# A longer weight ring from the output projection on, and the last six feature blocks run token tile by token tile

## The chip, the cores and the metric

The kernel runs on all 8 cores of one Trainium2 chip, each core on its own share of the tokens, with no communication between cores. The metric is the device time in microseconds (us) of the slowest core.

The engines of a core have these short names: PE is TensorE (matmul), PEld its weight loads, DVE is VectorE, ACT is ScalarE, POOL is GpSimd and SP is SyncE. POOL and SP do no arithmetic here; they only issue DMAs.

## What is computed

One layer of a diffusion backbone on 16 context sequences of 256 tokens and 4 latent sequences of 2048 tokens, model width 2048. The part that the change touches is the end of the layer and the final norm. The reference, cut to it:

```python
def _rmsnorm(x, g):
    xf = x.astype(jnp.float32)
    y = xf * lax.rsqrt(jnp.mean(xf * xf, axis=-1, keepdims=True) + EPS)
    return (y * g.astype(jnp.float32)).astype(x.dtype)

def _layer(x, cond, h0, n_chunks, p):
    ...
    mix = jnp.concatenate([rg_out, ch_out], axis=-1) @ p['w_out']
    x = x + gate1 * mix
    h2 = _rmsnorm(x, p['norm2_g']) * (1.0 + scale2) + shift2
    ff = jnp.square(jax.nn.relu(h2 @ p['w_ff1'])) @ p['w_ff2']    # 2048 -> 8192 -> 2048
    x = x + gate2 * ff
    return x, ...

y_prompt = _rmsnorm(xp, final_g)
y_sample = _rmsnorm(xs, final_g)
```

The products run in bfloat16 with float32 sums; x, the norms and the outputs are float32.

## The kernel before

Each core owns 1536 tokens. Activations lie with features on the 128 partitions and tokens along the free dimension, so the model width of 2048 is 16 feature blocks `f` of 128. From the output projection on, the 1536 tokens are two groups `g` of 768 (`GRP`), and each group is two token tiles, `TILES = ((0, 512), (512, 256))`: first 512 tokens, then 256.

**Stages.** In order of the program: norm 1 and the first modulation blocks; the recurrent half (`oth_...`, `own_...`); the chunk-mixing half; `out_proj(0, ...)` and `out_proj(1, ...)`, which also sum up the squares for norm 2; then for each group `g` and each half `hf` of the 8192 hidden features, 16 blocks of the first feed-forward product (`ff1`, with weights of 16x256 columns) and 16 of the second (`ff2`, one feature block each, 32 accumulated products for each token tile). In the first `ff1` stage, after blocks 4 to 11, `mod_block(5, ...)` puts eight small products with a weight block of `w_ada` in between. After `ff2` with `hf == 1` the group is finished: final norm and store of 16 feature blocks.

**Weights.** All weight blocks come through one ring in SBUF, `RING`, of `NUNIT = 8` units of 4096 bytes a partition. A block of `w_out`, `w_ada`, `w_ff1` or `w_ff2` takes two units, so four blocks fit. A first pass over the program records the order of use. `acquire` hands the next block out, `release` frees it after its last product, and both call `ring_issue`, which issues the next load on POOL's queue as soon as `ring_free` finds room. A load's start therefore waits for the release of the block that it overwrites. The loads convert float32 in HBM to bfloat16 in SBUF.

**One `ff2` block before.** For each token tile: 32 products into one PSUM bank (`bank()` goes round over 8 banks), then on DVE `stt` adds the gated product to `xA` (the residual, float32), and with `hf == 1` `stat_add` squares it on ACT into `sq` and adds it on DVE to `ss`. Then the block is released.

**The end of a group before.** `stat_end` multiplies `ss` by a matrix of ones on PE for both tiles (a sum over partitions), takes the square root on ACT into `rs`, and one reciprocal on DVE over all 768 columns. Then DVE scales the 16 blocks of `xA` in place (768 columns each), and SP issues one store of 384 KB behind each. In group 0 this stands ahead of the evictions of group 1's first products on DVE; in group 1 nothing follows it.

**Order.** Every engine runs its instructions in the order in which this Python code calls them; the `Tracker` puts semaphore waits ahead of them from the byte ranges that they read and write. All matmuls are recorded at line 154, all DMAs at 173, activations at 309, `ts` at 314 and 316, `tt` at 319, `stt` at 323 and the reciprocal at 333.

**Memory around the change.** `X16` is a region of 16384 bytes a partition. It held x tiles, then parts of the recurrent buffers and the two buffers `gu[0]` and `gu[1]`, which the last chunk-mixing products read. From `out_proj` on nothing in the kernel before uses it.

Of the kernel before, what the change touches and what calls it, by code (L numbers as in the profile page):

```python
# [11 lines left out]
DM = 2048  # L12
# [193 lines left out]
def emit(nc, order):  # L206
# [145 lines left out]
    head = [0]  # L352
    live = []
    nxt = [0, 0]

    def ring_place(n):
        p = head[0]
        if p + n > NUNIT:
            p = 0
        return p  # L360

    def ring_free(p, n):
        used = sum(u for _, _, u in live)
        if not live:
            return True
        span = set()
        for _, q, u in live:
            span.update(range(q, q + u))
        return not any(k in span for k in range(p, p + n)) and used + n <= NUNIT

    def ring_issue():
        if order is None:
            return
        while nxt[0] < len(order):
# [3 lines left out]
            if not ring_free(p, n):  # L378
                free = [q for q in range(0, NUNIT - n + 1) if ring_free(q, n)]
# [3 lines left out]
            tile = at(RING + p * UNIT, [128, shp[0], shp[1]], BF16, "w_" + key[0])  # L383
# [6 lines left out]
    def acquire(kind, i):  # L390
        key = (kind, i)
        if order is None:
# [4 lines left out]
            return at(RING + p * UNIT, [128, shp[0], shp[1]], BF16, "w_" + kind), len(rec) - 1  # L397
# [446 lines left out]
    nbank[0] = 8  # L844

# [23 lines left out]

    def stat_end():  # L870
        for o_, n_ in TILES:
            p = bank()
            T.mm([(p[:, 0:n_], ones_f[:, :], ss[:, o_:o_ + n_], True, True)])
            act(rs[:, o_:o_ + n_], p[:, 0:n_], AF.Sqrt, bias=cst[:, 0:1], scale=1.0 / DM)
        recip(rs[:, :], rs[:, :])
# [40 lines left out]
    for g in range(2):  # L916
        for hf in range(2):
# [14 lines left out]
            if g == 1 and hf == 0:  # L932
                for f in range(16):
                    T.dma("sp", xA[:, f, :], x1s[f], f"xl{f}", ins=[f])
            for f in range(16):
                w, n = acquire("ff2", hf * 16 + f)
                for ti, (o_, n_) in enumerate(TILES):
                    p = bank()
                    T.mm([(p[:, 0:n_], w[:, k, :], aT[:, k, o_:o_ + n_], k == 0, k == 31) for k in range(32)])
                    x_ = xA[:, f, o_:o_ + n_]  # L940
                    stt(x_, p[:, 0:n_], ec(modT, 5, f, te(g, ti)), x_, ALU.mult, ALU.add)
                    if hf == 1:
                        stat_add(x_, f == 0, o_, n_)
                release(n)
        stat_end()
        for f in range(16):
            stt(xA[:, f, :], xA[:, f, :], pkc("FG", f), rs[:, :], ALU.mult, ALU.mult)
            T.dma("sp", y_own[f * 128:(f + 1) * 128, g * GRP:(g + 1) * GRP], xA[:, f, :], f"y{f}", final=True)
# [144 lines left out]
```

How the kernel before makes its waits and increments, by code:

```python
    def need(self, eng, tok):  # L72
        if tok is None:
            return
        sid, val, src = tok
        if eng == "pe" and src == "pe":
            return
        if self.waited[eng].get(sid, 0) >= val:
            return
        self.waited[eng][sid] = val
        h = self.sems[sid]
        self.q[eng].append(lambda E, h=h, v=val: E.wait_ge(h, v))
# [50 lines left out]
    def op(self, eng, fn, ins, outs):  # L133
        i = [r for a in ins for r in self.runs(a)]
        o = [r for a in outs for r in self.runs(a)]
        self._deps(eng, i, o)
        t = self.tick(eng)
        h = self.sems[self.toks[t][0]]
        self.q[eng].append(lambda E, fn=fn, h=h: fn(E).then_inc(h, 1))
        self._mark(t, eng, i, o)
# [12 lines left out]
            def thunk(E, m=m, last=(k == n - 1), h=h):  # L153
                ins = E.matmul(m[0], lhsT=m[1], rhs=m[2], start=m[3], stop=m[4])
                if last:
                    ins.then_inc(h, 1)
# [5 lines left out]
    def dma(self, q, out, in_, key, ins=(), outs=(), final=False):  # L162
# [5 lines left out]
        d = self.dsem[key]  # L168
        d[1] += 16
        tok = (d[0], d[1], "dma")
        self.toks.append(tok)
        h = self.sems[d[0]]
        self.q[q].append(lambda E, o=out, i=in_, h=h: E.dma_start(out=o, in_=i).then_inc(h, 16))
        self._mark(len(self.toks) - 1, "dma", i, o)
        if final:
```

## Time and profile before

| | value |
|---|---|
| three runs of the kernel | 2239.37, 2242.27, 2596.65 us (median 2242.27) |
| the profiled execution, its time | 2239.04 us |
| its span on the slowest core (core 4) | 2237.2 us |
| spans of the eight cores | 2230.4 to 2237.2 us |
| PE busy, share of the span | 2084.1 us, 93% |
| DVE, ACT, POOL busy | 37%, 26%, 6% |
| chain that ended last: share of PE, DMA, DVE, ACT | 80%, 7%, 7%, 3% |
| granted TensorE clock, mean of the span | 0.970 of full speed |
| DMA moved | 285.73 MB, mean 128 GB/s |

The span goes from the first to the last instruction of a core; the time of an execution is some 2 us more. The third run, at 2596.65 us, was disturbed and is left aside. The chain that ended last is the sequence of work followed back from the last instruction; what is not on it was hidden beside something else. In the views by window, "PEclk" is the granted clock of TensorE (1.00 is 2.4 GHz, 0.50 is 1.2 GHz) and "DMA share" the busy share of the core's 16 DMA engines.

### The profile page before, as it was taken

How to read it: one execution, taken by the hardware profiler on the slowest of the kernel's cores; microseconds unless marked ns; L12 is line 12 of the kernel's file. 1: busy time of each engine (PE TensorE's matmuls, PEld its weight loads, DVE VectorE, ACT ScalarE, POOL GpSimd, SP SyncE). 2: the span in 40 equal slices, each digit the busy share in tenths (PEclk: the TensorE clock that was granted, in tenths of full speed). 3: DMA queues.
4: the chain of work that ended last, by engine and by line, in shares of the span. 5: the costliest groups of instructions: out<-in, count | busy, mean ns of one | idle time of the engine just before them, and what ended most of it. 6: DMA issues, size and time to landing. Idle time of an engine off the chain costs nothing.

```text
span 2237.2 us, 33122 instructions; the slowest of 8 cores (2230.4 to 2237.2 us)
## 1 busy us (share of the span) xinstructions
PE 2084.1 (93%) x13264; PEld 1217.7 (54%) x13264; DVE 833.0 (37%) x1151; ACT 577.6 (26%) x853; POOL 131.7 (6%) x243
## 2 busy tenths in 40 slices
PE   5776979999999999999999999999999999999994
PEld 4553434444445565555666555655565656665652
DVE  3545889985214566321111221225221111221224
ACT  3347778884111212111000111111111000111100
POOL 0000101100000000000000000000000000000000
PEclk9877979999999999999999999999999999999997
DMA  9998848779329786896655656557975656556553
GB/s 239 251 183 141 131 76 124 121 120 184 57 43 206 151 177 119 142 172 112 107 99 102 106 95 105 103 98 148 216 159 102 105 95 105 103 99 106 98 94 113
DMA packets 50405, 285.73 MB, mean 128 GB/s; under 512 B 5840, under 2 KB 6992, under 8 KB 23888
## 3 DMA queue, kind: packets, MB, share of 16 engines
q0 software_dynamic: 34416, 224.15, 61.0%
q1 hardware_dynamic: 15840, 59.48, 8.1%
q8 instruction: 108, 1.77, 0.3%
q14 instruction: 41, 0.34, 0.1%
HBM read 488.85 MB, written 18.89 MB: 227 GB/s over the span
## 4 chain that ended last, share of the span: by engine, by line
PE 80%; DMA 7%; DVE 7%; ACT 3%; issue 3%; DVEq 0%; ACTq 0%; SPq 0%; POOLq 0%
PE ps L154 80%; DMA w_ada<-w_ada 3%; DMA w_ff<-w_ff 2%; DMA xso<-x_oth 2%; DVE xA L323 1%; DVE xB L323 1%; ACT sq L309 1%; DVE oxc L323 1%; ACT L309 1%; DVE h2T L319 1%; ACT TA L309 0%; ACT MH L309 0%; DVE rs L333 0%; ACT TI L309 0%; DVE h2T L316 0%
## 5 line engine op out<-in xcount | busy, mean ns | idle before, releaser
L154 PE MATMUL ps<-h2T,w_ff 128*128 128x512 bf16 (+1 forms) x4096 | 670.1, 326 | 7.0 <-DMA w_ff<-w_ff 5.5
L154 PE MATMUL ps<-aT,w_ff 128*128 128x512 bf16 (+1 forms) x4096 | 666.3, 326 | 0.0
L154 PEld LDWEIGHTS ps<-h2T,w_ff 128*128 128x128 bf16 x4096 | 400.8, 98 | 274.4 <-issue 11.0
L154 PEld LDWEIGHTS ps<-aT,w_ff 128*128 128x128 bf16 x4096 | 400.8, 98 | 264.8
L309 ACT ACTIVATE aT<-ps 128x512 bf16<-128x512 f32 (+1 forms) x256 | 124.9, 490 | 889.3 <-DVE ps L314 889.2
L314 DVE TENSOR_SCALAR ps<-ps 128x512 f32<-128x512 f32 (+1 forms) x256 | 144.0, 565 | 483.5 <-PE ps L154 483.5
L323 DVE SCALAR_TENSOR_TENSOR xA<-ps,modT,xA 128x512 f32<-128x512 f32 (+1 forms) x160 | 98.6, 616 | 532.1 <-PE ps L154 532.1
L173 POOL DMA_DIRECT2D w_ff<-w_ff x128 | 67.8, 530 | 1262.0 <-PE ps L154 1249.3
L309 ACT ACTIVATE sq<-xA 128x512 f32<-128x512 f32 x90 | 47.1, 523 | 343.6 <-DVE xA L323 343.6
L154 PE MATMUL ps<-sqo,ones 128*128 128x256 f32 (+1 forms) x352 | 83.8, 397 | 27.6 <-ACT sqo L309 20.2
L319 DVE TENSOR_TENSOR ss<-ss,sq 128x512 f32<-128x512 f32 x120 | 67.0, 558 | 93.7 <-ACT sq L309 93.7
L154 PE MATMUL ps<-hTo,w_x 128*128 128x512 bf16 (+1 forms) x384 | 76.0, 355 | 24.0 <-DVE hTo L316 24.0
L154 PE MATMUL ps<-hT,w_x 128*128 128x512 bf16 x384 | 86.7, 383 | 9.6 <-ACT TA L309 8.2
L154 PE MATMUL ps<-gy,w_out 128*128 128x256 bf16 (+1 forms) x512 | 93.6, 326 | 1.0 <-DVE modT L319 1.0
L154 PE MATMUL ps<-cho,w_out 128*128 128x256 bf16 (+1 forms) x512 | 93.7, 326 | 0.0
L154 PEld LDWEIGHTS ps<-sqo,ones 128*128 128x128 f32 x352 | 71.4, 215 | 38.6 <-issue 28.9
L154 PE MATMUL ps<-hT,w_u 128*128 128x512 bf16 x384 | 84.5, 379 | 5.0 <-ACT TA L309 3.2
L154 PE MATMUL ps<-hT,w_y 128*128 128x512 bf16 x384 | 84.2, 379 | 0.0
L154 PE MATMUL ps<-w_v,hT 128*128 128x512 bf16 x384 | 83.2, 379 | 0.0
L154 PEld LDWEIGHTS ps<-gy,w_out 128*128 128x128 bf16 x512 | 50.0, 98 | 34.4 <-issue 1.5
L154 PEld LDWEIGHTS ps<-cho,w_out 128*128 128x128 bf16 x512 | 50.1, 98 | 33.1
L154 PEld LDWEIGHTS ps<-hT,w_x 128*128 128x128 bf16 x384 | 36.8, 98 | 57.0 <-issue 15.8
(107 smaller groups left out, 1332.7 us busy)
## 6 DMA issues: line engine op xcount, KB each, us to landing
w_ff<-w_ff POOLq DMA_DIRECT2D x128, 1024.0 KB, 9.8
w_ada<-w_ada POOLq DMA_DIRECT2D x48, 1024.0 KB, 15.9
w_out<-w_out POOLq DMA_DIRECT2D x16, 1024.0 KB, 11.0
xso<-x_own SPq DMA_DIRECT2D x6, 2048.0 KB, 17.3
y_own<-xA SPq DMA_DIRECT2D x32, 384.0 KB, 5.7
xso<-x_oth SPq DMA_DIRECT2D x4, 2048.0 KB, 24.2
w_x<-w_x POOLq DMA_DIRECT2D x16, 512.0 KB, 17.6
xA<-x_res SPq DMA_DIRECT2D x16, 384.0 KB, 19.3
```

What stands on the lines that cost most here:

```text
L154: ins = E.matmul(m[0], lhsT=m[1], rhs=m[2], start=m[3], stop=m[4])
L173: self.q[q].append(lambda E, o=out, i=in_, h=h: E.dma_start(out=o, in_=i).then_inc(h, 16))
L309: T.op("act", lambda E: E.activation(out=out, in_=in_, func=func, **kw), ins, [out])
L314: T.op("dve", lambda E: E.tensor_scalar(out=out, in0=in0, scalar1=a, scalar2=None, op0=op0), ins, [out])
L319: T.op("dve", lambda E: E.tensor_tensor(out=out, in0=in0, in1=in1, op=op), [in0, in1], [out])
L323: T.op("dve", lambda E: E.scalar_tensor_tensor(out=out, in0=in0, scalar=scalar, in1=in1, op0=op0, op1=op1), ins, [out])
```

## The change

It has three parts.

1. After the chunk-mixing stage the ring gets four more units, which lie in `X16`; `unit_at` gives their addresses, and `ring_place` sees to it that no block straddles the two regions. So from `out_proj(0, ...)` to the end six blocks of weights fit instead of four.
2. `stat_end` is cut into `stat_tile`, which does sum, square root and reciprocal for one token tile. The one reciprocal of 768 columns is now one of 512 and one of 256, in all four places where a norm ends.
3. In the last `ff2` stage (`g == 1`, `hf == 1`) the first ten blocks run as before. The last six are all acquired and held: first all six with tile 0 (512 tokens), then `stat_tile` of tile 0, then all six with tile 1 (256 tokens), each released after that. Behind the tile 1 evictions of the second to fifth of them, DVE gets four scalings of 512 columns each and SP four stores of 256 KB; so all 16 stores of tile 0 are issued in this second pass. At the end come `stat_tile` of tile 1, 16 scalings of 256 columns and 16 stores of 128 KB.

The arithmetic is the same, and so is the number of products.

```diff
@@ -366,7 +372,7 @@
-        return not any(k in span for k in range(p, p + n)) and used + n <= NUNIT
+        return not any(k in span for k in range(p, p + n)) and used + n <= nunit[0]
@@ -376,11 +382,11 @@
-            tile = at(RING + p * UNIT, [128, shp[0], shp[1]], BF16, "w_" + key[0])
+            tile = at(unit_at(p), [128, shp[0], shp[1]], BF16, "w_" + key[0])
@@ -842,6 +848,8 @@
     mod_late()
     nbank[0] = 8
+    nunit[0] = NUNIT + 4
+    ring_issue()
@@ -867,12 +875,15 @@
+    def stat_tile(o_, n_):
+        p = bank()
+        T.mm([(p[:, 0:n_], ones_f[:, :], ss[:, o_:o_ + n_], True, True)])
+        act(rs[:, o_:o_ + n_], p[:, 0:n_], AF.Sqrt, bias=cst[:, 0:1], scale=1.0 / DM)
+        recip(rs[:, o_:o_ + n_], rs[:, o_:o_ + n_])
+
     def stat_end():
         for o_, n_ in TILES:
-            p = bank()
-            T.mm([(p[:, 0:n_], ones_f[:, :], ss[:, o_:o_ + n_], True, True)])
-            act(rs[:, o_:o_ + n_], p[:, 0:n_], AF.Sqrt, bias=cst[:, 0:1], scale=1.0 / DM)
-        recip(rs[:, :], rs[:, :])
+            stat_tile(o_, n_)
@@ -932,20 +943,43 @@
+            def y_out(f, o_, n_, key):
+                x_ = xA[:, f, o_:o_ + n_]
+                stt(x_, x_, pkc("FG", f), rs[:, o_:o_ + n_], ALU.mult, ALU.mult)
+                a = g * GRP + o_
+                T.dma("sp", y_own[f * 128:(f + 1) * 128, a:a + n_], x_, f"{key}{f}", final=True)
+
+            last = g == 1 and hf == 1
+            for f in range(10 if last else 16):
+                w, n = acquire("ff2", hf * 16 + f)
+                for ti in range(2):
+                    ff2_tile(f, w, ti)
+                release(n)
+            if last:
+                held = [acquire("ff2", hf * 16 + f) for f in range(10, 16)]
+                for ti in range(2):
+                    for j in range(6):
+                        ff2_tile(10 + j, held[j][0], ti)
+                        if ti == 1:
+                            release(held[j][1])
+                            for f in range(4 * (j - 1), 4 * j) if 0 < j < 5 else ():
+                                y_out(f, *TILES[0], "y")
+                    stat_tile(*TILES[ti])
+                for f in range(16):
+                    y_out(f, *TILES[1], "z")
```

`ff2_tile` holds the body of the old loop over the tiles, word for word. At the end of group 0 `stat_end` and 16 scalings of 768 columns stand as before.

**PE, the end of the program.** In the kernel before, each of the last six `w_ff` blocks (numbers 324 to 329) is used for 512 and then 256 tokens; `ones` is the matrix that sums `ss` over partitions. The last blocks of the kernel before:

```order
L154 MATMUL ps<-aT_239,w_ff_327_369 128x512 x32
L154 MATMUL ps<-aT_239,w_ff_327_369 128x256 x32
L154 MATMUL ps<-aT_239,w_ff_328_370 128x512 x32
L154 MATMUL ps<-aT_239,w_ff_328_370 128x256 x32
L154 MATMUL ps<-aT_239,w_ff_329_371 128x512 x32
L154 MATMUL ps<-aT_239,w_ff_329_371 128x256 x32
L154 MATMUL ps<-ss_189,ones_48 128x512
L154 MATMUL ps<-ss_189,ones_48 128x256
```

And at the seam of the two passes after the change:

```order
L154 MATMUL ps<-aT_241,w_ff_328_370 128x512 x32
L154 MATMUL ps<-aT_241,w_ff_329_371 128x512 x32
L154 MATMUL ps<-ss_191,ones_48 128x512
L154 MATMUL ps<-aT_241,w_ff_324_366 128x256 x32
L154 MATMUL ps<-aT_241,w_ff_325_367 128x256 x32
```

The sum over `ss` of tile 0 now stands directly behind the last 512-token products, with five blocks' 256-token products moved behind it.

**DVE, the second pass.** Before, this place held only evictions (`xA<-ps`) and sums (`ss<-ss,sq`), and at the end one reciprocal and 16 scalings of 768 columns:

```order
L319 TENSOR_TENSOR ss_189<-ss_189,sq_187 128x512
L323 SCALAR_TENSOR_TENSOR xA_185<-ps,modT_44,xA_185 128x256
L319 TENSOR_TENSOR ss_189<-ss_189,sq_188 128x256
L333 RECIPROCAL rs_190<-rs_190 128x768
L323 SCALAR_TENSOR_TENSOR xA_185<-xA_185,pk_43,rs_190 128x768 x16
```

After the change, from the last eviction of tile 0 on:

```order
L319 TENSOR_TENSOR ss_191<-ss_191,sq_190 128x512
L333 RECIPROCAL rs_192<-rs_192 128x512
L323 SCALAR_TENSOR_TENSOR xA_187<-ps,modT_44,xA_187 128x256
L319 TENSOR_TENSOR ss_191<-ss_191,sq_189 128x256
L323 SCALAR_TENSOR_TENSOR xA_187<-ps,modT_44,xA_187 128x256
L319 TENSOR_TENSOR ss_191<-ss_191,sq_190 128x256
L323 SCALAR_TENSOR_TENSOR xA_187<-xA_187,pk_43,rs_192 128x512 x4
```

The reciprocal of 512 columns stands ahead of the first eviction of the second pass, and each of four evictions has four scalings behind it, ahead of the next eviction.

**POOL, the start of the longer ring.** The rows are loads of the output projection's weights; before, the fifth load (223) was issued behind the release of a block by PE:

```order
L173 DMA w_out_184<-w_out 128x4096
L173 DMA w_out_223<-w_out 128x4096
L173 DMA w_out_224<-w_out 128x4096
```

After the change:

```order
L173 DMA w_out_184<-w_out 128x4096
L173 DMA w_out_185<-w_out 128x4096
L173 DMA w_out_186<-w_out 128x4096
L173 DMA w_out_225<-w_out 128x4096
```

The fifth and sixth blocks are issued ahead of the output projection into the new units, and from there on each load is issued two blocks earlier than before.

## Rows read from the trace of the kernel before

**Rows 1.** Windows: length, then each engine's busy us (instructions), PEclk, DMA share, GB/s

```profile
932.00:1000.00 68.00, 62.46 (x510) 38.24 (x508) 15.23 (x31) 10.19 (x21) 6.32 (x12) 0.97 1.02 172
...
1720.00:2040.00 320.00, 320.00 (x1975) 192.96 (x1973) 54.28 (x93) 30.95 (x63) 16.42 (x31) 1.00 0.60 103
```

**Rows 2.** Waits of PE, 680 to 2240 us: total, times, longest

```profile
PE ps L154 <- DVE ss L319: 7.1, 5, 3.8
PE ps L154 <- DMA w_ff<-w_ff: 5.5, 5, 1.8
PE ps L154 <- DVE ps L314: 1.4, 1, 1.4
```

**Rows 3.** Timeline of POOL's load issues: start, us, what, idle before and releaser

```profile
909.57 0.53 POOL L173 DMA_DIRECT2D w_ff<-w_ff  x1 [9.81 <-PE ps L154]
...
1007.12 0.53 POOL L173 DMA_DIRECT2D w_ff<-w_ff  x1 [11.77 <-PE ps L154]
```

**Rows 4.** DMA issues, 900 to 1000 us: size, median us to landing

```profile
w_ff<-w_ff POOLq DMA_DIRECT2D x10, 1024.0 KB, 13.5
```

**Rows 5.** Windows around two stops of PE, columns as in rows 1

```profile
849.90:853.60 3.70, 0.00 (x0) 0.00 (x0) 2.15 (x5) 1.05 (x2) 0.53 (x1) 1.00 0.70 201
853.60:858.60 5.00, 4.93 (x13) 1.93 (x14) 3.81 (x8) 1.35 (x3) 0.00 (x0) 0.66 0.95 134
...
946.00:950.00 4.00, 4.00 (x12) 1.47 (x11) 0.00 (x0) 0.00 (x0) 0.00 (x0) 0.57 1.04 176
```

**Rows 6.** Timeline of the end of the span

```profile
2203.28 0.75 DVE L323 SCALAR_TENSOR_TENSOR xA<-ps,modT,xA 128x512 f32<-128x512 f32 x1 [5.33 <-PE ps L154]
...
2204.91 0.69 DVE L319 TENSOR_TENSOR ss<-ss,sq 128x512 f32<-128x512 f32 x1 [0.88 <-ACT sq L309]
...
2206.50 1.02 PE L154 MATMUL ps<-ss,ones 128*128 128x512 f32 x2
2206.77 0.48 DVE L323 SCALAR_TENSOR_TENSOR xA<-ps,modT,xA 128x256 f32<-128x256 f32 x1 [1.17 <-PE ps L154]
...
2207.73 0.67 ACT L309 ACTIVATE rs<-ps,cst 128x512 f32<-128x512 f32 x1
2207.92 0.42 DVE L319 TENSOR_TENSOR ss<-ss,sq 128x256 f32<-128x256 f32 x1 [0.67 <-ACT sq L309]
...
2209.84 4.95 DVE L333 RECIPROCAL rs<-rs 128x768 f32<-128x768 f32 x1 [1.49 <-ACT rs L309]
2214.89 14.95 DVE L323 SCALAR_TENSOR_TENSOR xA<-xA,pk,rs 128x768 f32<-128x768 f32 x16
2216.30 14.15 SPq L173 DMA_DIRECT2D y_own<-xA  x16
```

**Rows 7.** Groups on DVE by shape: busy us, mean ns, idle before

```profile
L333 DVE RECIPROCAL rso<-rso 128x256 f32<-128x256 f32 x10 | 17.5, 1753 | 71.3 <-ACT rso L309 71.3
...
L323 DVE SCALAR_TENSOR_TENSOR OTI<-OTI,oxc 128x1024 f32<-128x1024 f32 x8 | 9.7, 1214 | 0.0
```

**Rows 8.** DMA, 2206 to 2238 us: GB/s in 40 slices of 0.8 us

```profile
GB/s 0 0 0 0 0 0 0 0 0 0 0 0 0 41 388 396 392 403 396 396 376 369 357 319 311 330 330 380 384 349 334 307 319 357 373 246 23 0 0 0
```

**Rows 9.** Stores of the end: ns of an issue, us to landing; two small loads

```profile
L173 SPq DMA_DIRECT2D y_own<-xA x16: 332/335/656, 2216.3 to 2229.9; - x16
...
DMA to landing us min/median/max: 2.7/4.8/6.3
...
pk<-pk SPq DMA_DIRECT2D x1, 174.0 KB, 2.5
xst<-x_tail SPq DMA_DIRECT2D x1, 32.0 KB, 2.5
```

**Rows 10.** Timeline of the end of group 0

```profile
1538.04 0.67 ACT L309 ACTIVATE rs<-ps,cst 128x512 f32<-128x512 f32 x1
...
1540.15 4.95 DVE L333 RECIPROCAL rs<-rs 128x768 f32<-128x768 f32 x1 [1.49 <-ACT rs L309]
...
1561.71 13.58 PE L154 MATMUL ps<-h2T,w_ff 128*128 128x512 bf16 x78 [1.43 <-DVE ps L314]
```

More of the change, by code:

```diff
@@ L352, in emit, with unit_at @@
     head = [0]
+    nunit = [NUNIT]
     live = []
     nxt = [0, 0]
+    def unit_at(p):
+        return RING + p * UNIT if p < NUNIT else X16 + (p - NUNIT) * UNIT
     def ring_place(n):
         p = head[0]
-        if p + n > NUNIT:
+        if p < NUNIT < p + n:
+            p = NUNIT
+        if p + n > nunit[0]:
             p = 0
@@ L378, in ring_issue @@
             if not ring_free(p, n):
-                free = [q for q in range(0, NUNIT - n + 1) if ring_free(q, n)]
+                free = [q for q in range(0, nunit[0] - n + 1) if not q < NUNIT < q + n and ring_free(q, n)]
                 if not free:
@@ L396, in acquire @@
             head[0] = p + n
-            return at(RING + p * UNIT, [128, shp[0], shp[1]], BF16, "w_" + kind), len(rec) - 1
+            return at(unit_at(p), [128, shp[0], shp[1]], BF16, "w_" + kind), len(rec) - 1
         n = nxt[1]
@@ L934, in emit @@
                     T.dma("sp", xA[:, f, :], x1s[f], f"xl{f}", ins=[f])
-            for f in range(16):
[L936 to L948, printed above, removed]
+            def ff2_tile(f, w, ti):
+                o_, n_ = TILES[ti]
+                p = bank()
+                T.mm([(p[:, 0:n_], w[:, k, :], aT[:, k, o_:o_ + n_], k == 0, k == 31) for k in range(32)])
+                x_ = xA[:, f, o_:o_ + n_]
+                stt(x_, p[:, 0:n_], ec(modT, 5, f, te(g, ti)), x_, ALU.mult, ALU.add)
+                if hf == 1:
+                    stat_add(x_, f == 0, o_, n_)
@@ new lines, in y_out @@
+            def y_out(f, o_, n_, key):
+                x_ = xA[:, f, o_:o_ + n_]
+                stt(x_, x_, pkc("FG", f), rs[:, o_:o_ + n_], ALU.mult, ALU.mult)
[7 more added lines that the diff above has]
+                release(n)
@@ L949, in emit @@
+        if g == 0:
+            stat_end()
+            for f in range(16):
+                y_out(f, 0, GRP, "y")
     T.finish()
```

## The prediction

> **What bounds the kernel now.** I read the windows first. In the long feed-forward stages PE is busy for the whole of a window, 320 us of 320, at a granted clock of 1.00 and with the DMA engines at a share of 0.60 [rows 1]. There neither a deeper ring nor another order of loads can bring anything: PE does the same products after the change. What can move is only where PE stands still, and what lies behind its last product. So I read the waits of PE from 680 us on, where the output projection begins. Three kinds matter: five waits for `w_ff` loads, 5.5 us; five for sums into `ss`, 7.1 us, of which the longest is 3.8; and one for DVE, 1.4 us [rows 2]. The windows put the waits for loads into 932 to 1000 us, where PE is busy for 62.46 of 68 us and the DMA share is 1.02, that is full, at 172 GB/s [rows 1]. Last I read the end of the span: the last product is evicted at 2206.77, and the span ends at 2237.2, so 30.4 us have no product in them. They hold the sum and the root, a reciprocal of 4.95 us, 16 scalings in 14.95 us and the landing of the last stores [rows 6].
>
> **The longer ring.** The waits for loads fall where `mod_block(5)` puts a block of `w_ada`, which PE uses for hardly a microsecond, behind each `w_ff` block. Two blocks of 1 MB are then wanted for every 11.3 us or so, and at 172 GB/s a block takes 1049 KB / 172 = 6.1 us, two 12.2 us. So the loads fall behind by about 1 us per pair, for 8 pairs. From the release of `ff1` block 4 at 909.57 to that of block 12 at 1007.12 it takes 97.55 us [rows 3]. With four blocks in the ring a `w_ff` load is issued at a release and is wanted some 12 us later, and its median landing is 13.5 us [rows 4]: no slack. With six blocks it is wanted one more pair later, 23 to 24 us after its issue. The deficit of 8 x 1 us does not use up the 11 us gained. I take all five waits as gone, 5.5 us. After one of them the clock fell as well: 946 to 950 has 0.57 [rows 5], which is (1 - 0.57) x 4 = 1.7 us of PE's time. Together **-7.0 us**. Bounds: nothing, if waits come back elsewhere, and -7.2. The two extra loads at the start are taken from a stage in which PE waits for no load at all, so I cost them at nothing; uncovered they would be 2 x 6.1 us.
>
> **The cut reciprocal.** At the end of group 0 the reciprocal of 768 columns starts at 1540.15, behind both roots. The one of 512 can start when the first root ends, 1538.04 + 0.67 = 1538.71 [rows 10]. A reciprocal of 256 columns takes 1.75 us [rows 7] and one of 768 4.95 us [rows 6], so 6.25 ns a column and 3.35 us for 512. Both are done at about 1543.9 instead of 1545.1, 1.2 us earlier. The scalings behind them hold up the evictions of group 1 until PE has no bank left and waits 1.43 us [rows 10]; of this **-1.2 us** go. In the other places no PE wait hangs on the reciprocal: nothing. Bounds 0 and -1.4.
>
> **The seam of the two passes.** I count from the start of the eviction of the last 512-token tile (2203.28 in the rows). Its sum into `ss` ends 2204.91 + 0.69 - 2203.28 = 2.3 us later. Before, PE meanwhile had 256-token products to do. Now the sum over partitions of tile 0 stands next in PE's queue, and all second-pass products are queued behind it. PE stands still for 2.4 us and then spends 1.0 us on that sum (1.02 in the row): it begins the second pass at 3.4. **+3.4 us.**
>
> **DVE in the second pass.** One 256-token block takes PE 2206.77 - 2203.28 = 3.49 us. DVE needs for each: from the eviction's start to the end of its sum 2207.92 + 0.42 - 2206.77 = 1.57 us, and four scalings. The 16 of 768 columns follow each other every 14.95 / 16 = 0.934 us; 256 columns more or less make 0.69 - 0.42 = 0.27 us [rows 6]; the 1024-column operation of the same kind takes 1.21 us [rows 7], which fits. So 0.67 us for 512 and 0.40 for 256. Four scalings are 2.7 us, and with the 1.57 a block costs DVE 4.24 us: **more than PE's 3.49**. First comes the reciprocal of 512, from 4.3 to 7.7. The evictions could start at 6.9, 10.4, 13.9, 17.4, 20.8 and 24.3; they start at 7.7, 10.4, 14.7, 18.9, 23.1 and 27.4. PE does not stop, since it has 8 banks, but the last eviction is **3.05 us** late. Its sum ends at 28.95. In the kernel before it would, on the same count, end 5.06 us after the last large tile's eviction plus five 256-token passes (17.45), at 22.5. The step costs 6.45 us in all.
>
> **The tail.** Before, from the end of that sum (2208.34) to the last scaling's end (2229.84) it is 21.5 us. After: 1.5 to the start of the reciprocal as before, 1.75 for it, 0.1, and 16 x 0.40 = 6.4, together 9.75: **-11.75 us**. SP keeps up with one store per 0.40 us, since an issue takes it 0.33 us [rows 9]. From the last scaling to the end it is 7.4 us now. The stores are fed at 384 KB per 0.934 us, 421 GB/s, and leave at 300 to 400 GB/s until about 2235 [rows 8]: they are late by then. After the change they are fed at 131 KB per 0.40 us, 328 GB/s, which these rates can take away, so the last one lands in about the shortest time of such a store, 2.7 us [rows 9]. I take 4.4 us for this end, **-3.0 us**; bounds -3.6 and, see below, a loss.
>
> **The clock at the seam.** The 2.4 us stop is a risk of its own. After a stop of 3.7 us PE ran at 0.66 for 5 us, and after one of 1.3 us at 0.57 for 4 us, either time 1.7 us lost; after most of the short ones it did not fall [rows 5]. Since the slowest of eight cores counts, I take **+1.7 us**, bounds 0 and 2.
>
> **The sum.** -7.0 - 1.2 + 6.45 - 11.75 - 3.0 + 1.7 = -14.8 us on the profiled execution's 2239.0: 2224.2. The median of the runs is 3.2 us above that execution, and one undisturbed run is at its level, so I add half of that: **2226 us**. That is 0.7% less. A change within 2% is about what a measurement of this kernel cannot tell from none.
>
> **Rivals.**
> *The stores of 128 KB cost by their pieces, not by their bytes.* A store writes 128 rows; they were 3 KB long and are now 1 KB. If a piece costs as much as before, the last 16 stores take as long as the 16 before, some 18.7 us from the first issue. That issue comes at 2216.3 + 6.45 + 1.7 - 3.2 - 0.5 = 2220.7, so the end is at about 2241.4 instead of 2237.2: the tail then loses 4 us instead of gaining, and the time is 2237. For it: nothing in the trace has such a store. Against it: a load of 174 KB in pieces of 1.4 KB and one of 32 KB in pieces of 256 bytes both land in 2.5 us [rows 9].
> *The stores do not overlap.* This is the case on the slower side. If each 128 KB store held the queue for its own 2.7 us, 16 would take 43 us from 2220.7, and the end would be near 2266: 2261 us in all with the other gains. It would decide from 1.4 us a store on. Against it: 16 stores of three times the size took only 18.7 us, with landings of 2.7 to 6.3 us each, so several are in flight. The Trainium skill, "DMA: Bandwidth & Descriptors", sections on the anatomy of one DMA and on bandwidth, speaks against small stores: about 2.0 us fixed for each plus bytes / 436 GB/s, and the advice to batch to 1 MiB. By this an estimate is 2.3 us for 128 KB and 36.8 us for 16 one after another; but it would make 46 us of the 16 old ones, and the trace shows under 19. Only a fixed part that is paid once at the end agrees with the rows.
> *The waits for loads stay.* At a DMA share of 1.02 the loads are bound by rate, and a longer ring only delays the first wait. If the loads are slower than 6.1 us a block once two more are in flight, from about 6.6 us on, the cushion is used up, and the time goes towards 2233.
> *The seam is cheaper.* No fall of the clock, and DVE's operations overlap more than their rows show: 2220 to 2222.
>
> **How the numbers follow.** The forecast 0.55, with its own range of 2221 to 2231. Seam cheaper 0.13. Waits for loads stay 0.12 (2233). Stores by pieces 0.10 (2237). Stores one by one 0.03 (2261). Other mixtures 0.07. The range 2218 to 2238 holds all but the last two. None but a disturbed measurement is outside 2%: faster 0.01, same 0.98, slower 0.01.
>
> **What would show it.** In the new trace: no PE wait for `w_ff` between 900 and 1010, and the issues of the releases of `ff1` blocks 4 and 12 some 90 us apart instead of 97.55. One PE wait for `ss` of about 2.4 us some 45 us before the end, and the clock behind it. DVE without gaps between the second and the sixth 256-column eviction, and the last of them about 3 us behind its product. A reciprocal of 256 columns of 1.75 us, 16 scalings in 6.4 us, and 4 to 5 us from there to the end. A PE wait of about 0.2 us instead of 1.43 at the start of group 1. I am wrong if PE waits appear in the output projection, if a wait for loads is left, or if the end behind the last scaling is longer than 7 us.

## The result

| | before | after |
|---|---|---|
| median | 2256.17 us (21 runs) | 2240.72 us (21 runs) |
| fastest run | 2239.37 us | 2228.56 us |
| ratio | 1 | 0.993, 95% interval [0.9900, 0.9959] |
| profiled execution: time, span | 2239.04, 2237.2 us (core 4) | 2230.77, 2229.2 us (core 6) |
| spans of the eight cores, mean | 2234.6 us | 2224.5 us |

The change makes the kernel 0.7% faster, which is what was forecast as a ratio (2226 to 2242.27 is 0.993), but the time that was forecast, 2226 us with a range up to 2238, is missed: the median is 2240.72. Here and in the sets below some executions had a lower granted clock on some cores and took some 10 to 390 us longer: the medians contain them, the ratios leave out only the longest of them, and the times given for the experiments leave out all of them. Of the 21 runs of the changed kernel nine lie at 2228.56 to 2230.77 us, of the 21 of the kernel before eight at 2239.37 to 2245.49.

The waits of PE from 680 us on, core 6 of the changed kernel. Against [rows 2] the waits for `w_ff` are gone, the 1.4 us for DVE have become 0.3, and the waits for `ss` have grown from 7.1 to 13.0:

```profile
PE ps L154 <- DVE ss L319: 13.0, 7, 4.4
...
PE ps L154 <- ACT aT L309: 0.3, 1, 0.3
```

The window in which the waits for loads lay, to be read against the first of [rows 1] (those are of core 4, on which this stage begins 4.5 us earlier than on core 6 here); PE is busy for 67.54 instead of 62.46 of 68 us at a clock of 1.00, while the DMA engines are as full as before:

```profile
932.00:1000.00 68.00, 67.54 (x576) 42.71 (x580) 17.73 (x35) 11.78 (x24) 6.36 (x12) 1.00 1.02 168
```

POOL's issues at the releases of `ff1` blocks 4 and 12, against [rows 3]. They are 89.38 us apart instead of 97.55:

```profile
914.10 0.54 POOL L173 DMA_DIRECT2D w_ff<-w_ff  x1 [10.05 <-PE ps L154]
...
1003.48 0.53 POOL L173 DMA_DIRECT2D w_ff<-w_ff  x1 [9.83 <-PE ps L154]
```

The last stage in the timeline of core 6, in place of [rows 6]:

```profile
2180.85 0.75 DVE L323 SCALAR_TENSOR_TENSOR xA<-ps,modT,xA 128x512 f32<-128x512 f32 x1 [4.58 <-PE ps L154]
...
2183.32 2.05 PE L154 MATMUL ps<-ss,ones 128*128 128x512 f32 x2 [2.58 <-DVE ss L319]
...
2185.16 21.74 PE L154 MATMUL ps<-aT,w_ff 128*128 128x256 bf16 x192
...
2186.89 3.35 DVE L333 RECIPROCAL rs<-rs 128x512 f32<-128x512 f32 x1 [3.71 <-ACT rs L309]
2190.16 0.39 DVE L323 SCALAR_TENSOR_TENSOR xA<-ps,modT,xA 128x256 f32<-128x256 f32 x1
...
2193.03 0.48 DVE L323 SCALAR_TENSOR_TENSOR xA<-ps,modT,xA 128x256 f32<-128x256 f32 x1 [1.40 <-PE ps L154]
...
2194.52 2.73 DVE L323 SCALAR_TENSOR_TENSOR xA<-xA,pk,rs 128x512 f32<-128x512 f32 x4
...
2205.45 0.48 DVE L323 SCALAR_TENSOR_TENSOR xA<-ps,modT,xA 128x256 f32<-128x256 f32 x1
...
2209.59 0.48 DVE L323 SCALAR_TENSOR_TENSOR xA<-ps,modT,xA 128x256 f32<-128x256 f32 x1
...
2210.73 0.42 DVE L319 TENSOR_TENSOR ss<-ss,sq 128x256 f32<-128x256 f32 x1 [0.67 <-ACT sq L309]
...
2211.30 1.19 PE L154 MATMUL ps<-ss,ones 128*128 128x256 f32 x2 [4.41 <-DVE ss L319]
...
2213.17 1.75 DVE L333 RECIPROCAL rs<-rs 128x256 f32<-128x256 f32 x1 [2.01 <-ACT rs L309]
2215.03 6.42 DVE L323 SCALAR_TENSOR_TENSOR xA<-xA,pk,rs 128x256 f32<-128x256 f32 x16
```

PE stops for 2.58 us ahead of the sum of tile 0, and that sum takes 2.05 us instead of the 1.02 of [rows 6]: the clock has fallen. DVE's evictions in the second pass have an idle time ahead of them only at the second; from then on the one gap of DVE in each block is the 0.67 us ahead of the sum into `ss`, in which it waits for the square on ACT. The last product was finished at about 2206.9 (2185.16 + 21.74), its eviction starts at 2209.59.

And the stores of tile 1, to be read against the first and second of [rows 9]: SP starts one every 0.49 us (7.3 us for 15), and they land in 1.8 us, yet the span ends at 2229.2, 7.75 us behind the last scaling (2215.03 + 6.42 = 2221.45) and 6.3 us after the issue of the last store:

```profile
L173 SPq DMA_DIRECT2D y_own<-xA x16: 333/402/412, 2215.6 to 2222.9; - x16
...
DMA to landing us min/median/max: 1.7/1.8/1.9
```

**Where the time went.** Cores start the output projection at different times (676 to 681 us in the kernel before, 676 to 684 after the change), so I compare stretches and not points in time. For each core I read four marks out of the timelines: PE's sum over `ss` for norm 2 of group 0, the same for the final norm of group 0, the last sum over `ss`, and the first of the last 16 scalings. The means over eight cores, in us:

| stretch | before | after | difference | forecast |
|---|---|---|---|---|
| norm 2 to final norm of group 0 | 771.07 | 764.15 | -6.9 | -7.0 |
| from there to the last sum | 671.68 | 677.58 | +5.9 | +6.95 (seam, lag of DVE, clock, less 1.2) |
| last sum to the first scaling | 6.40 | 3.70 | -2.7 | -3.2 |
| the 16 scalings | 14.95 | 6.42 | -8.5 | -8.55 |
| last scaling to the end of the span | 6.57 | 7.80 | **+1.2** | **-3.0** |
| sum | | | -11.0 | -14.8 |

The output projection of group 0 lies ahead of the first mark. It takes 85.4 us to that mark on the mean of the cores in both kernels, so the two extra loads cost nothing there. They are also not issued ahead of it, as the order of the program suggests. On core 6 PE begins it at 683.7, and POOL can issue them only 1.8 and 4.7 us later:

```profile
685.48 0.53 POOL L173 DMA_DIRECT2D w_out<-w_out  x1 [1.30 <-DVE ps L319]
688.42 0.53 POOL L173 DMA_DIRECT2D w_out<-w_out  x1 [2.41 <-DVE s L323]
```

### The profile page after: what moved, and what is told of

The parts are those of the page before. It is cut to its first block, busy times and chain, and to the rows that moved or that the text cites. A ratio compares the mean times of both kernels' runs of the same rounds, so it can differ in the third digit from the quotient of the medians.

```text
span 2229.2 us, 32991 instructions; the slowest of 8 cores (2220.0 to 2229.2 us)
## 1 busy us (share of the span) xinstructions
PE 2072.0 (93%) x13068; PEld 1219.0 (55%) x13264; DVE 835.1 (37%) x1171; ACT 577.7 (26%) x853; POOL 129.8 (6%) x243
## 4 chain that ended last, share of the span: by engine, by line
PE 79%; DVE 11%; DMA 4%; issue 4%; ACT 2%; DVEq 0%; ACTq 0%; SPq 0%; POOLq 0%
PE ps L154 79%; DMA w_ada<-w_ada 2%; DMA xso<-x_oth 1%; DVE uxc L323 1%; DVE xA L323 1%; DVE MH L327 1%; DVE TI L319 1%; DVE TI L323 1%; DVE oxc L323 1%; ACT sq L309 1%; DVE MH L316 0%; DVE MH L319 0%; DVE xB L323 0%; ACT L309 0%; DVE hT L319 0%
## 5 line engine op out<-in xcount | busy, mean ns | idle before, releaser
L154 PE MATMUL ps<-h2T,w_ff 128*128 128x256 bf16 (+1 forms) x4032 | 662.9, 325 | 4.0 <-ACT aT L309 0.3
L309 ACT ACTIVATE sq<-xA 128x512 f32<-128x512 f32 (+1 forms) x90 | 47.1, 523 | 347.3 <-DVE xA L323 347.3
L319 DVE TENSOR_TENSOR ss<-ss,sq 128x512 f32<-128x512 f32 (+1 forms) x120 | 67.0, 559 | 93.5 <-ACT sq L309 93.5
L154 PEld LDWEIGHTS ps<-hTo,w_x 128*128 128x128 bf16 x384 | 32.3, 107 | 66.9 <-issue 45.2
```

Source lines behind the costliest of these rows:

```text
L154: ins = E.matmul(m[0], lhsT=m[1], rhs=m[2], start=m[3], stop=m[4])
L309: T.op("act", lambda E: E.activation(out=out, in_=in_, func=func, **kw), ins, [out])
L319: T.op("dve", lambda E: E.tensor_tensor(out=out, in0=in0, in1=in1, op=op), [in0, in1], [out])
```

## The experiments

Each ratio is to the kernel before, run beside it, where it took 2240 to 2247 us. The stretches are those of the table above, means over the eight cores.

### One half of the change alone

**The longer ring alone**, in the kernel before (`unit_at` and the new `ring_place` go with it, and are left out here):

```diff
     nbank[0] = 8
+    nunit[0] = NUNIT + 4
+    ring_issue()
```

> The kernel before with the longer ring alone (six blocks from the output projection on). Theory: the waits for w_ff loads and the clock fall behind one of them go, and nothing else moves. From the sum for group 0's second norm to that for its final norm each core took 769.6 to 772.5 us before; I expect 764 to 765 as in the changed kernel, no PE wait for w_ff, the tail as before (7.4 us behind the last scaling), and a time 7 to 8 us under the kernel before, ratio 0.997. Rival: the shorter stretch came from the cut reciprocal or from chance between executions; then 770 to 772 us and no difference in time.

Measured: 2233.4 to 2237.7 us, ratio 0.9951 [0.9922, 0.9980]. The first stretch is 764.49 us, between 764.1 and 764.8 on all cores; everything behind it is as before (671.69, 6.40, 14.96), and the end is 6.67 us. In PE's waits of core 6 (680 to 2240 us) none is for `w_ff`:

```profile
PE ps L154 <- DVE ss L319: 7.1, 5, 3.9
PE ps L154 <- ACT aT L309: 1.6, 1, 1.6
PE ps L154 <- DVE modT L319: 1.0, 1, 1.0
PE ps L154 <- DVE h2T L316: 0.2, 1, 0.2
```

So the ring gives its 6.6 us by itself, and the cut reciprocal has no part in it. PE's wait at the start of group 1, which the reciprocal holds up, stays at 1.4 to 1.65 us on every core here; only with the cut does it go.

**The last stage alone.** The changed kernel, with the ring made longer only at the last stage:

```diff
     nbank[0] = 8
-    nunit[0] = NUNIT + 4
-    ring_issue()
...
             last = g == 1 and hf == 1
+            if last:
+                nunit[0] = NUNIT + 4
+                ring_issue()
```

> The changed kernel, but the ring is longer only from the last stage on; before that four blocks as in the kernel before. Theory: the waits for w_ff loads are back (3.9 to 6.5 us a core, the stretch between the two sums of group 0 at 770 to 772 us), the last stage is as in the changed kernel: 48.4 us from the last 512-token eviction to the end. Time 4 to 5 us under the kernel before (3 us from the last stage, 1.1 from the reciprocal at the end of group 0). Rival: the held blocks need the long ring well ahead of the stage; then PE waits for loads inside the first pass and the time is at or above the kernel before.

Measured: 2234.9 to 2239.9 us, ratio 0.9979 [0.9942, 1.0016]; the interval contains 1, so by the time of the whole kernel alone this half is not told from nothing. The stretches do tell it: 771.60 us (no gain), then 677.03, 3.70, 6.42 and 7.81 as in the changed kernel, 4.6 us less than before in the sum of these four. The waits for loads are back, here in core 0:

```profile
PE ps L154 <- DVE ss L319: 12.8, 6, 4.4
PE ps L154 <- DMA w_ff<-w_ff: 6.1, 4, 2.4
```

The two halves add up: -6.6 and -4.6 give -11.2, the changed kernel has -11.0.

### The end behind the last store

After the trace it was open what fills 7.8 us behind the last scaling when a store lands in 1.8. `T.finish()` makes SP wait for the last value of every DMA semaphore that it has not waited for and for the engines: 107 waits in the changed kernel, 91 in the one before (16 semaphores more for the second set of stores). A wait that is already met should cost little; the question is whether a hundred of them do. The view of line 82, on which all waits stand, has them in the changed kernel, core 6, behind the last store:

```profile
L82 SPq EVENT_SEMAPHORE  x107: 17/17/17, 2223.3 to 2229.0; - x107
```

Each is listed with 17 ns, but the 107 take 5.7 us, 53 ns from one start to the next. The last store has landed by 2224.7 (2222.9 + 1.8), so over 4 us of the row have nothing else beside them. I moved all that can be waited for earlier to a place where SP has nothing else to do; no wait is dropped.

```diff
+    def settle(self):
+        for sid, cnt in self.dsem.values():
+            self.need("sp", (sid, cnt, "dma"))
...
                     stat_tile(*TILES[ti])
+                    if ti == 0:
+                        T.settle()
```

> The changed kernel, with SP's final waits for all DMAs issued until then moved ahead of the stores of tile 0, where SP is idle; only the waits for the 32 stores and the engines stay at the end. Theory: the 7.75 us between the last scaling and the end are not the landing of the last store (1.8 us) but some 90 waits that SP works through one after another; with 55 ns each about 4 us go, the end is 3.5 to 4 us behind the last scaling and the time 4 us under the changed kernel, 16 to 17 under the kernel before. Rival: the end is a fixed cost behind the last landing; then the 7.7 us stay and the time is that of the changed kernel.

Measured: 2224.2 to 2227.2 us, against 2228.6 to 2230.8 of the changed kernel; ratio 0.9908 [0.9876, 0.9941]. The end is 4.33 us instead of 7.80, with 34 waits left. Core 6, from the timeline, ends its scalings at 2212.64 + 6.42 = 2219.06:

```profile
2212.64 6.42 DVE L327 SCALAR_TENSOR_TENSOR xA<-xA,pk,rs 128x256 f32<-128x256 f32 x16
```

Its span, from the view of the cores, ends 4.1 us later:

```profile
core 6: 2223.2 us, clock 0.970
```

Its 16 stores of tile 1 land in the same time as in the changed kernel or a little more, so it is not the landing that got shorter:

```profile
DMA to landing us min/median/max: 1.7/1.8/2.4
```

What stands behind the last store now is 34 waits in 1.8 us:

```profile
L82 SPq EVENT_SEMAPHORE  x34: 17/17/17, 2221.2 to 2223.0; - x34
```

73 waits fewer and 3.47 us less are 48 ns for a wait that is met, near the 53 of the row.

The same in the kernel before, `T.settle()` ahead of the last 16 stores:

> The kernel before, with SP's final waits moved ahead of the last 16 stores. Theory: there the waits run beside the landing of stores that are queued up (4.8 us median), so moving them gives 0 to 1.5 us: last scaling to end 6 to 7.4 us. Rival (fixed cost of every wait at the end, not hidden): 4 us less, as in the changed kernel.

Measured: 2238.9 to 2240.9 us, ratio 0.9970 [0.9944, 0.9995]; the end is 5.32 us instead of 6.57. With the same 73 waits fewer only 1.25 us go. In core 6 the scalings end at 2214.41 + 14.96 = 2229.37, and the span is 2234.7 us (2227.36 and 2234.4 before, 7.1 us):

```profile
2214.41 14.96 DVE L327 SCALAR_TENSOR_TENSOR xA<-xA,pk,rs 128x768 f32<-128x768 f32 x16
```

So in the kernel before most of the row of waits ran beside the landing of queued stores (median 4.8 us, [rows 9]); the change took that cover away. A gain of 3 us in the landing was paid for by waits that had been hidden.

### The seam and the lag of DVE

**Work under the stop.** The norm of tile 0 behind the first block of the second pass:

```diff
                     for j in range(6):
                         ff2_tile(10 + j, held[j][0], ti)
                         if ti == 1:
                             release(held[j][1])
+                            if j == 0:
+                                stat_tile(*TILES[0])
...
-                    stat_tile(*TILES[ti])
+                stat_tile(*TILES[1])
```

> The changed kernel, but the sum over partitions, root and reciprocal of tile 0 stand behind the first 256-token block of the second pass instead of ahead of it. Theory: PE has work while the sum into ss is made, so its stop of 2.5 us at the seam and the fall of the clock behind it (1.5 us, on five of the eight cores) go. From the last 512-token eviction to the start of the last sum over partitions, 28.0 us on the cores with the fall and 26.5 us on those without, I expect 24.9 to 25.9 us on all, because DVE is the slower one in the second pass and its reciprocal moves up by 1 us less than PE's stop. Time 1.5 to 3 us under the changed kernel. Rival: DVE alone sets the second pass and the stop was hidden under it; then the stretch stays at 26.5.

Measured: 2227.3 to 2228.3 us, ratio 0.9929 [0.9916, 0.9941]; the stretch to the last sum is 674.98 us on every core. In the changed kernel it is 676.61 on three cores and 678.15 on the other five, so 1.6 us and 3.2 us go. (The 28.0 and 26.5 us of the expectation are counted from the start of the first sum, 2.5 us behind the eviction that it names.) On core 6 PE goes on without a stop, and the sum of tile 0 takes 1.02 us:

```profile
2181.50 1.02 PE L154 MATMUL ps<-ss,ones 128*128 128x512 f32 x2
2182.36 17.63 PE L154 MATMUL ps<-aT,w_ff 128*128 128x256 bf16 x160
2205.57 1.19 PE L154 MATMUL ps<-ss,ones 128*128 128x256 f32 x2 [5.58 <-DVE ss L319]
```

Beside it a core of the changed kernel on which the clock did not fall (core 4), where PE stops as long but its sum takes 1.10 us:

```profile
2176.25 1.10 PE L154 MATMUL ps<-ss,ones 128*128 128x512 f32 x2 [2.58 <-DVE ss L319]
```

The fall of the clock behind the 2.58 us stop is thus worth 1.5 us and came on five cores of eight. But of PE's stop of 2.58 us only 1.6 us come back on the cores without the fall, because DVE is the one that sets the second pass: PE then waits 5.58 us for the last sum instead of 4.41.

**Fewer scalings per block.** Three behind each eviction, the last four behind the last sum:

```diff
-                            for f in range(4 * (j - 1), 4 * j) if 0 < j < 5 else ():
+                            for f in range(3 * (j - 1), 3 * j) if 0 < j < 5 else range(12, 16) if j == 5 else ():
```

> The changed kernel with three instead of four scalings behind each of the second to fifth 256-token evictions, and the last four behind the last sum, in the gap in which DVE waits for PE and ACT. Theory: with 1.57 + 3 x 0.67 = 3.6 us a block DVE keeps up with PE (3.49), so the last eviction starts 2 us earlier and the last sum over partitions too; 0.7 us of that is given back because four scalings take 2.7 us and the gap has 2.0. 1.4 us off the time. Rival: the lag of DVE does not reach the end; then nothing.

Measured: 674.86 us to the last sum (-2.7) and 4.27 us from there to the first scaling (+0.6), together -2.1 where 1.4 was expected: PE's wait for the last sum falls from 4.41 to 1.83 us. The times of the whole kernel (2228.6 to 2229.2 us, ratio 0.9933 [0.9915, 0.9951]) do not resolve it. The lag of DVE is real and reaches the end. Another mend was not tried. From eviction to eviction DVE takes 4.14 us (2205.45 to 2209.59), of which 0.67 are the gap ahead of the sum, and a scaling of 512 columns takes 0.67. By these numbers one scaling placed between the eviction and the sum would bring a block with four scalings to an estimated 3.5 us, PE's pace.

### How many blocks the ring needs

The kernel before with five blocks, `nunit[0] = NUNIT + 2` and otherwise the edit of the longer ring alone:

> The kernel before with a ring of five blocks from the output projection on instead of four or six. Theory: the loads fall behind by about 1 us for each of 8 pairs, and one more block puts the issue of a load one more step ahead (10 us every second time, 1 us the other), so the deficit of 8 us is just covered: 764 to 765.5 us between the two sums of group 0, at most one short wait. Rival: only two more blocks help, as the short step of 1 us decides; then some waits stay, 767 to 770 us.

Measured: 2236.4 to 2239.2 us, ratio 0.9973 [0.9963, 0.9983]; the first stretch is 767.39 us, 766.5 to 768.1 on the cores. My expectation was wrong, and the rival's number holds: one more block gives half of the gain (3.7 of 6.9 us). In core 2 three waits are left, the last at 996 us:

```profile
972.82 10.56 PE L154 MATMUL ps<-h2T,w_ff 128*128 128x512 bf16 x64 [0.49 <-DMA w_ff<-w_ff]
...
996.75 18.57 PE L154 MATMUL ps<-h2T,w_ff 128*128 128x512 bf16 x109 [1.03 <-DMA w_ff<-w_ff]
```

The landing times show why. These are the `w_ff` loads issued from 935 to 970 us with five blocks (core 2):

```profile
DMA to landing us min/median/max: 19.8/21.2/22.0
```

and those of the changed kernel with six (core 6):

```profile
DMA to landing us min/median/max: 14.3/15.8/18.8
```

In this region two blocks are released 0.8 us apart every 11.2 us, and two loads are issued. With six blocks the first of the two is a `w_ff` load, as in the rows of POOL above; with five it is the `w_ada` load, and the `w_ff` load queues behind it:

```profile
938.48 0.53 POOL L173 DMA_DIRECT2D w_ada<-w_ada  x1 [9.89 <-PE ps L154]
939.32 0.53 POOL L173 DMA_DIRECT2D w_ff<-w_ff  x1 [0.31 <-issue]
```

So the fifth block brings `w_ff` 10.4 us more time from issue to use (22.4 us), but its loads land about one block's load time later than with six. From 970 us on they take up to 24.6 us and are late; with six they have 23.2 us and land in 18.8 at most up to there. What was wrong in my expectation was to count the time that a deeper ring adds and to keep the landing time of the four-block ring, which is kept short by the very waits that are to go. That the order of the two loads makes the difference between five and six is read from these rows; it was not tried by itself.

### All mends together

The changed kernel with the three edits above (norm of tile 0 later, three scalings per block, waits early):

> The changed kernel with all three: the norm of tile 0 behind the first 256-token block, the scalings spread, SP's final waits moved ahead. Theory: 5.0 us (cores with the fall of the clock) or 3.5 us (cores without) and 3.6 us for the waits: 7 to 8.6 us under the changed kernel, 20 to 21 under the kernel before, about 2221. Rival: the three share one gain; then it is not faster than with the waits alone, some 3.5 us under the changed kernel.

Measured: 2221.2 to 2223.4 us, ratio 0.9906 [0.9892, 0.9919]. The stretches add up: 764.27, then 672.33, 4.27, 6.42 and 4.78, 7.7 us less than the changed kernel from the second on. No core has the fall of the clock at the seam. PE's wait and the two products of the last sum, core 6:

```profile
2206.24 0.67 PE L154 MATMUL ps<-ss,ones 128*128 128x256 f32 x2 [2.93 <-DVE ss L323]
```

The end of 4.78 us is 0.45 more than with the waits early alone. With the waits early SP falls further behind: on some cores (two with the waits early alone, six here) one of its last issues takes 0.6 to 2.6 us instead of 0.40, here on core 1:

```profile
L173 SPq DMA_DIRECT2D y_own<-xA x11: 332/403/2553, 2211.9 to 2219.2; - x11
```

In the changed kernel the longest on any core is 0.41. Where the longer issues come from was not found.

**Eight stores instead of sixteen at the end.** In the changed kernel DVE scales one block every 0.40 us at the end, but an issue takes SP 0.40 and the next starts only 0.49 us after it; so its last issue starts 1.5 us behind the last scaling, where it was 0.1 before. So, on top:

```diff
-                for f in range(16):
-                    y_out(f, *TILES[1], "z")
+                for f in range(16):
+                    x_ = xA[:, f, o_:o_ + n_]
+                    stt(x_, x_, pkc("FG", f), rs[:, o_:o_ + n_], ALU.mult, ALU.mult)
+                    if f % 2:
+                        T.dma("sp", y_own[(f - 1) * 128:(f + 1) * 128, a:a + n_].rearrange("(k p) t -> p k t", p=128),
+                              xA[:, f - 1:f + 1, o_:o_ + n_], f"z{f}", final=True)
```

> The kernel of e6_all_mends with the 16 stores of tile 1 joined to 8 of 256 KB, one behind every second scaling. Theory: at the end SP issues a store every 0.40 us and its last issue comes 1.5 us behind the last scaling; with half as many it comes 0.1 to 0.4 us behind it, and 16 semaphores less are waited for: 1 to 1.5 us less between the last scaling and the end (4.8 us in the mean of the cores). Rival: the landing of the last, larger store takes the gain back; then the same within 0.5 us.

Measured: 2217.7 and 2226.9 us, ratio 0.9907 [0.9870, 0.9943]; the profiled execution took 2326.88 us and is not read. It was run again beside the kernel of all mends; the changed kernel was run again too:

> The kernel of e9_mends_paired once more, since its profile and most of its executions were disturbed. Theory: 2.6 to 2.8 us from the last scaling to the end on every core, all stretches before as in e6_all_mends, and a time of 2218 to 2221 us, 1.5 to 2.5 us under e6_all_mends. Rival: the time of e6_all_mends.

> The kernel of e6_all_mends once more, beside the one above on the same chip: about 2222 us.

> The changed kernel once more, so that it is timed beside the version above on one chip. Theory: some 12 to 13 us under the kernel before, and 7 to 8 us above the version with all mends, whose stretches are 4.7 us shorter in the last stage and 3.0 us at the end. If it stands within 3 us of that version, the mends are worth less in time than in the trace.

Measured: the paired version 2218.3 to 2220.7 us, ratio 0.9878 [0.9837, 0.9920]; all mends 2219.8 and 2220.1 (only two runs, ratio 0.9894 [0.9838, 0.9950]); the changed kernel 2228.8 to 2230.8 (0.9945 [0.9910, 0.9979]). The end of the paired version is 2.71 us on the mean of the cores; that of all mends is 4.78 in its first trace and 4.36 in its second. Core 6 ends its scalings at 2208.17 + 6.42 = 2214.59 and its span at 2217.5:

```profile
2208.17 6.42 DVE L327 SCALAR_TENSOR_TENSOR xA<-xA,pk,rs 128x256 f32<-128x256 f32 x16
```

By the traces it is 1.7 to 2.1 us better. Its last issue starts 0.07 us behind the last scaling on every core, no issue takes over 0.39 us, and 26 waits stand behind it instead of 34; so the gain holds the longer issues of the version with all mends too. On core 6, where those have 0.41 at most, the end goes from 4.1 to 2.9 us. The larger stores land in 2.3 us instead of 1.8, so the rival of the first expectation has a part in it but does not take the gain back. That the paired version is also faster than all mends in the time of the whole kernel is likely but below what these runs resolve. Both are faster than the kernel before, by 1.1 to 1.2%, and 8 to 10 us faster than the changed kernel.

## Why the prediction was wrong, and where it was right

Two steps failed. One is a term of the sum, the end behind the last scaling, taken at -3.0 us and measured at +1.2. The other is the step from the profiled execution to the time, and it is the larger: it put the level of the kernel before at 2240.6 us, 15.5 below its median of 2256.17. The other terms came out within about 1 us each. The measured median lies 14.7 us above the forecast of 2226: 3 us of this show in the nine shortest runs of the changed kernel (middle one 2229.03), the other 11.7 lie between these and the median. With the end as it was measured the forecast would be 2230, and 2240.72 would still lie above the range up to 2238. So the end explains the missing gain, and the level explains why the time lies outside the range.

**The longer ring: right.** Forecast -7.0 us, measured -6.9 with the whole change and -6.6 alone. The mechanism was as told: no wait for `w_ff` is left, the clock stays at 1.00 in that window, and the releases of blocks 4 and 12 are 89.4 us apart where I had said some 90. The rival that the waits only move, because the loads are bound by rate, has fallen, though not by much: with one block less it would have been half right (3.2 of 6.9 us left). The two extra loads, costed at nothing, cost nothing: no wait for a load stands in the output projection.

**The cut reciprocal: right.** PE's wait at the start of group 1 was 1.43 us on six cores and 1.65 on cores 0 and 6, and is 0.11 and 0.33 now: 1.3 us less on every core, forecast 1.2. With the ring alone it stayed. The two reciprocals run from 1535.17 on behind one another, 4.96 us in all, and DVE's scalings start 7.1 us behind the sum of tile 0 (1533.17 to 1540.24) instead of 8.4 (1536.81 to 1545.20):

```profile
1535.17 4.96 DVE L333 RECIPROCAL rs<-rs 128x512 f32<-128x512 f32 x2 [0.15 <-ACT rs L309]
...
1556.96 8.38 PE L154 MATMUL ps<-h2T,w_ff 128*128 128x512 bf16 x46 [0.33 <-ACT aT L309]
```

**The seam: right in mechanism and nearly in size.** PE's stop was forecast at 2.4 us and is 2.58. I had the evictions of the second pass start at 7.7, 10.4, 14.7, 18.9, 23.1 and 27.4 us from the eviction of the last large tile, plus 1.7 if the clock falls; in core 6, where it fell, they start at 9.3, 12.2, 16.3, 20.5, 24.6 and 28.7. The last sum ends 30.3 us after that point, forecast 28.95 + 1.7. DVE's block takes 4.14 us, forecast 4.24. On the mean of the cores the stretch is 1.05 us shorter than forecast, mostly because three of the eight did not have the fall and the fall is 1.5 us instead of 1.7. Both parts are shown by removal: the stop and the fall by the filled seam, the lag by the spread scalings.

**Root, reciprocal and scalings: right** but for 0.5 us: the last sum takes 1.19 instead of 0.67 us behind PE's stop of 4.41 us. With the scalings spread (stop of 1.83 us) and with all mends (2.93 us) it took 0.67 again, so it is the clock behind the longer stop. The scalings take 6.42 us, forecast 6.4.

**The end behind the last scaling: wrong, and this is where the missing gain is.** The step said: "I take 4.4 us for this end, **-3.0 us**". It was 7.8 us, +1.2. I had looked only at the last store, and the 4.4 us are not worked out from a row: 2.7 of them are the landing, the rest has no name. The landing did get shorter, even more than I took: 1.8 us. But two things stood beside it that I did not cost. The larger is SP's row of waits at the end, 107 of them in 5.7 us, of which the landing hides 1.4 (2223.3 to 2224.7); moving 73 of them away gave back 3.5 us. In the kernel before I saw 7.4 us there, put it all down to the stores, and did not ask what else SP does in it, though `finish` stands in the code and the change adds 16 semaphores to it. The smaller is SP's pace: I said that it keeps up with one store per 0.40 us because an issue takes 0.33. At this pace an issue takes 0.40 and issues start 0.49 us apart, so the last one starts 1.5 us behind the last scaling; half as many stores, with 8 waits less, took that lag away.

**From the profiled execution to the time: wrong.** The sum went against one execution at 2239.0 us, and I set the level at half way between it and the median of three runs, 2242.27. Over 21 runs the median of the kernel before is 2256.17, so the level was 15.5 us too low, and my range was laid around a level that three runs do not fix; the third of them, 2596.65, I had left aside. The sum has no term for what the longer executions add to a median. As a difference the forecast is nearer: 14.8 us by the sum, 11.0 us by the stretches. That the ratio came out at the forecast 0.993 is in part luck: 11.0 of 2239 us are 0.995, and the same two kernels beside each other again gave 0.9945.

**The rivals.** That the stores of 128 KB cost by their pieces: no, 16 of them leave at one per 0.49 us, which is SP's pace, and land in 1.8. That they do not overlap: no, since at that pace three to four are in flight at once. The Trainium skill, "DMA: Bandwidth & Descriptors", section on the anatomy of one DMA, would give an estimate of 2.3 us for a store of 128 KB by its fixed 2.0 us and its rate, a fit for DMAs that GpSimd issues, while these are issued by SP; the trace has 1.8 us from issue to landing, and the sum of 16 such times is paid by none of the runs. That the seam is cheaper: partly, on the three cores without the fall of the clock.

## What to carry to other kernels

When a tail is shortened, ask what else ran under it: here a row of 107 waits, each already met, became the end of the kernel, and moving them to an idle place on their queue was worth as much as a third of the whole change. Ahead of a pass that is meant to hide work, add up what the hiding engine has to do per block and compare it with the block: 4.24 us against 3.49 us could be worked out beforehand from the rows, and three scalings instead of four, with the rest in a gap, mended it. A time needs more runs than a difference: cost a change as a difference, and give its level a range of its own from the spread of the kernel before.

## What was not expected of the hardware

A semaphore wait of SP that is already met costs about 50 ns (73 of them, 3.47 us by removal; 107 in 5.7 us by the row of line 82). The timeline leaves such waits out: in it the last DMA issue starts at 2222.9, and nothing is listed from there to 2229.2. Each is recorded with only 17 ns. The Trainium skill, "Perfetto Trace Analysis", section on the per-instruction lifecycle, says that a sequencer's time in a semaphore wait lies outside the window that the profiler reports; the trace agrees in so far as 17 ns are recorded of about 50, and it does not show what fills the rest.

A stop of PE of 2.58 us lowered the granted clock to 0.50 on five of eight cores, in one and the same program, and not on the other three. The window behind it in core 6:

```profile
2183.00:2186.00 3.00, 2.68 (x6) 1.25 (x7) 0.18 (x1) 0.25 (x1) 0.00 (x0) 0.50 0.00 0
```

The traces of the other versions with this stop have it on five, four, four and two of eight cores (waits early, changed kernel again, scalings spread, last stage alone). So a cost of this kind is a chance per core. With the slowest of eight cores as the metric it is mostly paid: the slowest core had the fall in four of these five traces, and not in that of the last stage alone.

With loads bound by rate, the landing time of a load is no constant of the load: for the `w_ff` loads issued from 970 to 1000 us the median was 13.9 us with four blocks, 23.5 with five and 22.4 with six, at the same 168 to 172 GB/s over 932 to 1000 us.
